# Three-product matmul units of a hybrid decoder step, grouped by kind of product instead of by tile

## What is computed

```python
mixed = jax.nn.sigmoid(ga) * (o_a @ p['w_pa']) + jax.nn.sigmoid(gb) * (o_b @ p['w_pb'])
x = x + mixed @ p['w_o']
h2 = _rmsnorm(x, p['g_ffn'])
x = x + (jax.nn.silu(h2 @ p['w_gate']) * (h2 @ p['w_up'])) @ p['w_down']
...
y = _rmsnorm(x, g_final)
```

## Time and profile before

| | |
|---|---|
| runs | 2039.28, 2046.54, 2046.58 us |
| the profiled execution | 2043.91 us, its span 2042.1 us |
| TensorE (PE) busy | 1995.0 us, 98% of the span, 15613 matmuls and as many weight loads |
| VectorE, ScalarE busy | 1064.3 us (52%), 732.6 us (36%) |
| mean granted TensorE clock | 0.988 |
| gate and up units, lines 1075 to 1077 | 3 x 1408 matmuls |
| down units, the same lines | 3 x 704 matmuls |
| mixing and output units, lines 1030 to 1032 | 3 x 768 matmuls |

### The profile page before, as it was taken

How to read it: one execution, slowest core, us unless ns; L and a number is a source line. 1 busy time by engine, 2 the same in 40 slices (tenths; PEclk the granted TensorE clock), 3 DMA queues, 4 the chain that set the end, 5 groups by cost and what they waited for, 6 DMA issues and landing times.

```text
span 2042.1 us, 38026 instructions
## 1 busy us (share of the span) xinstructions
PE 1995.0 (98%) x15613; PEld 1802.9 (88%) x15613; DVE 1064.3 (52%) x1272; ACT 732.6 (36%) x964; POOL 44.5 (2%) x63
## 2 busy tenths in 40 slices
PE   8999989999999999999999999999999999999996
PEld 7999766678875766699999999999999999999996
DVE  6655966378873520154445555444555555444444
ACT  6333101432233110144444444444444444333332
POOL 0000002200000000000000000000000000000000
PEclk9999998999999999999999999999999999999998
DMA  6444257344558898834446554444444444544443
GB/s 263 174 155 158 103 196 173 89 141 132 174 194 292 280 385 341 330 125 165 163 165 222 188 175 165 166 165 166 167 167 168 167 168 152 200 159 168 161 164 117
DMA packets 103625, 378.13 MB, mean 185 GB/s; under 512 B 26995, under 2 KB 36851, under 8 KB 76147
## 3 DMA queue, kind: packets, MB, share of 16 engines
q1 hardware_dynamic: 78802, 346.88, 48.6%
q0 software_dynamic: 4736, 18.80, 2.8%
q10 hardware_dynamic: 20000, 11.28, 2.0%
HBM read 359.30 MB, written 17.58 MB: 185 GB/s over the span
## 4 chain that ended last, share of the span: by engine, by line
PE 89%; DVE 4%; SPq 3%; DMA 2%; issue 1%; ACT 1%; DVEq 0%; ACTq 0%
PE ps L466 15%; PE ps L1075 14%; PE ps L1076 14%; PE ps L1077 13%; PE ps L1030 5%; PE ps L1032 5%; PE ps L1031 5%; PE ps L499 2%; PE ps L498 2%; PE ps L500 2%; PE ps L986 1%; PE ps L937 1%; SPq L359 1%; SPq L360 1%; PE ps L510 1%
## 5 line engine op out<-in xcount | busy, mean ns | idle before, releaser
L2003 DVE TENSOR_TENSOR weights_lo<-ring,weights_hi 128x2048 fp32r<-128x2048 f32 (+1 forms) x152 | 305.6, 2011 | 284.8 <-ACT weights_hi L1515 284.8
L1076 PE MATMUL ps<-h_lo,weights_hi 128*128 128x288 f32 x1408 | 416.1, 296 | 0.0
L1075 PE MATMUL ps<-h_hi,weights_hi 128*128 128x288 f32 x1408 | 414.6, 294 | 0.3 <-DVE weights_lo L2003 0.3
L1077 PE MATMUL ps<-h_hi,weights_lo 128*128 128x288 f32 x1408 | 412.5, 293 | 0.0
L1515 ACT ACTIVATE weights_hi<-ring 128x2048 fp32r<-128x2048 f32 (+1 forms) x152 | 257.1, 1691 | 365.9 <-PE ps L1077 356.8
L466 PE MATMUL ps<-hT,ring 128*128 128x288 f32 x1472 | 387.6, 416 | 0.0
L466 PEld LDWEIGHTS ps<-hT,ring 128*128 128x128 f32 x1472 | 276.7, 193 | 80.2 <-issue 7.1
L1077 PEld LDWEIGHTS ps<-h_hi,weights_lo 128*128 128x128 f32 x1408 | 265.1, 188 | 0.0
L1075 PEld LDWEIGHTS ps<-h_hi,weights_hi 128*128 128x128 f32 x1408 | 264.1, 188 | 0.6 <-DVE weights_lo L2003 0.6
L1076 PEld LDWEIGHTS ps<-h_lo,weights_hi 128*128 128x128 f32 x1408 | 264.4, 188 | 0.1
L1075 PE MATMUL ps<-act_hi,weights_hi 128*128 128x288 f32 x704 | 208.4, 296 | 0.0
(11 more groups left out here) (356 smaller groups left out, 2979.9 us busy)
## 6 DMA issues: line engine op xcount, KB each, us to landing
ring<-in_wst SPq DMA_DIRECT2D x209, 1024.0 KB, 4.9
ring<-in_wdn SPq DMA_DIRECT2D x64, 704.0 KB, 4.1
arena<-in_v SPq DMA_DIRECT2D x64, 512.0 KB, 5.5
arena<-in_kT SPq DMA_DIRECT2D x112, 256.0 KB, 5.6
arena<-chunk_ar_bk ACTq DMA_DIRECT2D x24, 256.0 KB, 3.9
arena<-in_ki SPq DMA_DIRECT2D x64, 64.0 KB, 1.9
arena<-in_kT SPq DMA_DIRECT2D x8, 512.0 KB, 6.5
arena<-in_xT SPq DMA_DIRECT2D x4, 592.0 KB, 6.7
```

The costliest lines, as they stand in the source:

```text
L1075: mm(out, W_HI[:, (u - U_FF) % 2, w], hi, start=start, stop=False)
L1076: mm(out, W_HI[:, (u - U_FF) % 2, w], lo, start=False, stop=False)
L1077: return mm(out, W_LO[:, u % 4, w], hi, start=False, stop=stop)
L2003: tt(W_LO[:, u % 4, 0:m], raw, W_HI[:, at, 0:m].bitcast(F32), ALU.subtract).then_inc(sem("w_split"), 1)
```

## The change

The three products of a unit are no longer issued tile by tile. Each unit now issues the high-by-high products of all its tiles, then all high-by-low, then all low-by-high. Only the first matmul of the whole group starts the bank and only the last one stops it. The number of matmuls, their operands, their banks and the counting of `unit_read` at a unit's end stay as they are. The waits inside a unit (`mix_h_split`, `mix_free`, `h_split`) stand ahead of the same tile's high-by-high product, as before. The numbers of lines move by one to three.

```diff
-            def mix_three(out, u, k, hi, lo, start, stop):
+            def mix_part(part, out, u, k, hi, lo, first, last):
                 w = slice(k * P, (k + 1) * P)
-                mm(out, MW_HI[:, (u - U_MIX) % 2, w], hi, start=start, stop=False)
-                mm(out, MW_HI[:, (u - U_MIX) % 2, w], lo, start=False, stop=False)
-                return mm(out, W_LO[:, u % 4, w], hi, start=False, stop=stop)
+                weights = W_LO[:, u % 4, w] if part == 2 else MW_HI[:, (u - U_MIX) % 2, w]
+                return mm(out, weights, lo if part == 1 else hi, start=(part == 0 and first), stop=(part == 2 and last))
...
-                    for k in range(KT):
-                        if s == 0 and k == KT - 1:
-                            pe.wait_ge(sem("mix_free"), KT + 2)
-                        ins = mix_three(ps[s % 2][:, 0:NT], U_O + s, k, MX_HI[:, k, :], MX_LO[:, k, :],
-                                        k == 0, k == KT - 1)
+                    for part in range(3):
+                        for k in range(KT):
+                            if s == 0 and k == KT - 1 and part == 0:
+                                pe.wait_ge(sem("mix_free"), KT + 2)
+                            ins = mix_part(part, ps[s % 2][:, 0:NT], U_O + s, k, MX_HI[:, k, :], MX_LO[:, k, :],
+                                           k == 0, k == KT - 1)
...
-                for k in range(KT):
-                    if first:
-                        pe.wait_ge(sem("h_split"), k + 1)
-                    ins = three(ps[(s + 2) % 4][:, 0:NT], U_FF + s, k, H_HI[:, k, :], H_LO[:, k, 0:NT],
-                                k == 0, k == KT - 1)
+                for part in range(3):
+                    for k in range(KT):
+                        if first and part == 0:
+                            pe.wait_ge(sem("h_split"), k + 1)
+                        ins = one(part, ps[(s + 2) % 4][:, 0:NT], U_FF + s, k, H_HI[:, k, :], H_LO[:, k, 0:NT],
+                                  k == 0, k == KT - 1)
```

More of the change, by code:

```diff
@@ L1038, in _ @@
                     pe.wait_ge(sem("mix_w_split"), i * 4 + (2 * s + 1))
-                    for k in range(KT):
-                        if s == 0 and k % 4 == 0:
-                            pe.wait_ge(sem("mix_h_split"), k // 4 + 1)
-                        ins = mix_three(ps[3 * s][:, 0:NT], u0, k, MH_HI[:, k, :], H_LO[:, k, 0:NT],
-                                        k == 0, k == KT - 1)
+                    for part in range(3):
+                        for k in range(KT):
+                            if s == 0 and k % 4 == 0 and part == 0:
+                                pe.wait_ge(sem("mix_h_split"), k // 4 + 1)
+                            ins = mix_part(part, ps[3 * s][:, 0:NT], u0, k, MH_HI[:, k, :], H_LO[:, k, 0:NT],
+                                           k == 0, k == KT - 1)
                     ins.then_inc(sem("unit_read"), 1)
                     pe.wait_ge(sem("mix_w_split"), i * 4 + (2 * s + 2))
-                    for part, (hi, lo) in enumerate(((OA_HI, OA_LO), (OB_HI, OB_LO))):
+                    for half, (hi, lo) in enumerate(((OA_HI, OA_LO), (OB_HI, OB_LO))):
                         if s == 0:
[L1048 to L1051, removed]
+                            pe.wait_ge(sem("branch_split"), half + 1)
+                        for part in range(3):
+                            for k in range(CT):
+                                ins = mix_part(part, ps[3 * s + 1 + half][:, 0:NT], u0 + 1, half * CT + k,
+                                               hi[:, k, :], lo[:, k, :], k == 0, k == CT - 1)
                     ins.then_inc(sem("unit_read"), 1)
@@ L1070, in squares_total, with one @@
                 mm(ps[7][:, 0:NT], ones, SQS, start=True, stop=True).then_inc(sem("squares_summed"), 1)
-            def three(out, u, k, hi, lo, start, stop):
+            def one(part, out, u, k, hi, lo, first, last):
                 w = slice(k * P, (k + 1) * P)
-                mm(out, W_HI[:, (u - U_FF) % 2, w], hi, start=start, stop=False)
-                mm(out, W_HI[:, (u - U_FF) % 2, w], lo, start=False, stop=False)
-                return mm(out, W_LO[:, u % 4, w], hi, start=False, stop=stop)
+                weights = W_LO[:, u % 4, w] if part == 2 else W_HI[:, (u - U_FF) % 2, w]
+                return mm(out, weights, lo if part == 1 else hi, start=(part == 0 and first), stop=(part == 2 and last))
             def gate_up(i, s, first=False):
@@ L1105, in down @@
                     pe.wait_ge(sem("w_split"), i * 8 + (2 * FT + 4 * t + q + 1))
-                    for k in range(FQ):
-                        ins = three(ps[4 + t][:, 0:NT], U_DOWN + 4 * t + q, k, A_HI[:, q * FQ + k, :],
-                                    A_LO[:, q * FQ + k, :], q == 0 and k == 0, q == 3 and k == FQ - 1)
+                    for part in range(3):
+                        for k in range(FQ):
+                            ins = one(part, ps[4 + t][:, 0:NT], U_DOWN + 4 * t + q, k, A_HI[:, q * FQ + k, :],
+                                      A_LO[:, q * FQ + k, :], q == 0 and k == 0, q == 3 and k == FQ - 1)
                     ins.then_inc(sem("unit_read"), 1)
```

## The result

The changed kernel takes 2051.95 us, median of 17 runs (2044.31 to 2059.45), against 2039.89 us for 17 runs of the kernel before (2036.94 to 2048.36). The ratio is 1.005, interval 1.0040 to 1.0061: slower by 8 to 12 us, an interval that lies clear of no change. The profiled execution took 2055.82 us with a span of 2054.0.

A forecast was written before the change was run, and what follows sets the result against it. TensorE was taken to bound the kernel. Stalls of 2.98 and 3.04, clock 3.2 and pace 5.6 summed to 14.8 us, giving 2058.7 on the profiled execution or 2061.3 on the median; forecast 2060 us, range 2047 to 2065.

The forecast's parts named there:

- the first rival: Only the stalls cost time, with clock or pace at most in part: 2050 to 2054 us, chance 0.35.
- Terms 1 and 2: TensorE stalls at the 16th matmul of the first output unit, 2.98 us, and first feed-forward gate unit, 3.04 us.
- Term 3: Behind each of the two stalls the clock drops for 3.4 us, costing 1.6 us each, 3.2 us together.
- Term 4: The 104 units reading `h_lo` slow by 0.054 us each, 5.6 us; output, branch and down units keep their pace.
- The rule on shared weights: Skill's rule that weights are loaded once and used repeatedly, so the old tile order would lose something; counted as nothing.
- The rival of a faster steady walk: Streaming one array in a row speeds all touched units' matmuls to, say, 130 ns: 2031 us, 13 us faster, chance 0.05.

The follow-up runs named there:

- x2: The kernel before, with only the output units with s = 0 and the first feed-forward gate unit by kind of product: 2050.62 us, ratio 1.0042.
- x12: The kernel before, all tile by tile, with only the two inner waits asked for at the 16th matmul of their units: 2048.12 us, ratio 1.0035.
- x1: The changed kernel with the output units with s = 0 and the first feed-forward gate unit tile by tile again: 2042.64 us, ratio 1.0003 to before.
- x6: The changed kernel with tile 15's three products last in the output units with s = 0 and first gate unit: 2044.87 us, ratio 1.0012 to before.
- x5: Several matmul orders by turns in each kind of unit; snake is by parts with high-by-low walked backwards. One profiled execution: 2044.81 us.
- x3: The kernel before, with only the 64 down units by kind of product: 2039.81 us, ratio 0.9995.
- x9: The kernel before, unaltered, profiled a second time: profiled execution of 2045.97 us.
- x7: The changed kernel, unaltered, profiled a second time: profiled execution of 2052.55 us.
- x10: The changed kernel, unaltered, profiled a fourth time: profiled execution of 2044.33 us.

## Why the prediction was right, and where its sum was not

- **Range and direction** held: 2051.95 us lies in 2047 to 2065, and the kernel is slower. The size was forecast too high, 14.8 us against 8 to 12, and the time lies in the band of the first rival, 2050 to 2054. Of the 8 us between it and the forecast of 2060 most are the base: the median of three runs, 2046.54 us, from which I added, was 6.7 us above that of 17. On 2039.89 the same sum gives 2054.7. That the range held in spite of it is owed to its width. (Its lower end is also not what its words give: the stalls on the lowest of the three runs are 2045.3, not 2047.)
- **Terms 1 and 2, the stalls: right**, place, cause and size. 2.98 and 3.04 us were worked out; the timelines give 2.97 for the first (9.36 us in x2 less the 6.39 of a unit without the wait) and 3.02 to 3.08 for the second. x2 and x12 show cause by putting them in, x1 and x6 by taking them out.
- **Term 3, the clock: a low stretch does come behind such a stall, but not each time.** I took "one drop per stall" from a single row of idle time, and that row's own drop is missing in 5 of 14 profiles. It came behind 5 of 12 stalls, at 1.5 us where 1.6 was worked out. The mean is 2 x 0.42 x 1.5 = 1.3 us, not 3.2 (with the changed kernel's own 5 of 8 it is 1.9). The range's lower end had room for it. The 1.6 us of idle time that I counted as a case without a drop says little: TensorE has only 0.7 us of work left behind it, and from 2029.5 us on, when it has stopped, the clock is low.
- **Term 4, the pace: two steps failed.** Gate and up units became slower, as forecast, but by 0.040 us, not 0.054: 4.1 us for 104 units, not 5.6. The reason, the steps of 1152 and 1184 bytes, isn't borne out: the snake of x5 has the same steps, only backwards in one part, and takes 6.33 us like the tile order. So the direction was in part luck. And "down units keep the walks of 1152 bytes and their 133.4 ns: 0" was wrong: they gained 0.043 us each, 2.8 us in all. The step took from one order of one stage that equal distances of addresses give an equal pace; x3 and x5 show that they don't (4.35 to 4.40 us for the 33 matmuls of a down unit). Net, the pace costs 1.3 us.
- With what the runs showed the sum is 6.0 + 1.3 + 4.1 - 2.8 = 8.6 us, within the measured 8 to 12. The difference of the two profiled executions, 11.9, holds two drops behind the stalls and a third at 880 us, which the kernel before can have as well (x9).
- **The rule on shared weights** had no part in it: the tile order, in which two products share a tile of weights, was 0.040 us better in gate and up units and 0.043 us worse in down units, so the runs show no steady gain from sharing them.
- **The rival of a faster steady walk** had a true core. The order did make down units faster, by 1.3 ns a matmul, and 130 ns did occur, but in one stage of one execution (x7), and not by the order.

## What to carry to other kernels

A regrouped loop can keep each inner wait at the same tile and still ask for it earlier in time. Count at which instruction each inner wait now stands, and compare its time with that at which the thing it waits for is ready. Here a wait for the last tile, with 1.1 to 1.2 us to spare at the 46th place of a unit, cost 3.0 us at the 16th, in two places, and taking those units out of the new order (x1), or just their last tile (x6), gave it back. And where a difference is under one per cent, profile the same kernel more than once: a low stretch of the clock or a faster pace may be that execution's own.

## What the runs showed of the hardware

- A unit of 48 matmuls, each 128x128 by 288 columns in fp32r, takes another time by the order of its matmuls: gate and up units 6.33 to 6.41 us, output units 6.36 to 6.44 (x5, before). Without waits, and with the clock at 1.00, that is 132 to 134 ns from start to start. But for the case below, a settled unit takes the same to 0.01 us in every profiled execution of the same program.
- The same output units of the changed kernel took 6.400 us each in three executions and 6.240 in a fourth, for 15 units in a row; it began behind a lower clock and ended at the next stall. What sets it stays open: no experiment aimed at it.
- Idle stretches of 2.7 to 2.8 us of TensorE are followed by 3.4 us at the lower level, 1.2 GHz, in 5 of 12 cases, and each costs 1.5 us. At 70 us an idle time of 2.0 to 2.8 us was followed by such a stretch in 9 of 14 executions, 2.10 us with one (before) and 2.25 without (x10). What decides was not settled.
